# Attention of two layers: products with the values turned round, two heads side by side, two tiles of queries at a time

## The reference, cut to what matters

```python
def causal_block_attention(q, k, v, log_decay=None):
    ...
        logits = jnp.einsum('bhqd,bhkd->bhqk', qc, k).astype(jnp.float32)
        if log_decay is not None:
            logits = logits + args[2][..., None] - log_decay[:, :, None, :]
        q_idx = i * Q_BLOCK + jnp.arange(Q_BLOCK)
        logits = jnp.where(key_idx[None, :] <= q_idx[:, None], logits, -jnp.inf)
        p = jax.nn.softmax(logits, axis=-1).astype(v.dtype)
        return jnp.einsum('bhqk,bhkd->bhqd', p, v)
```

## Time and profile before

| | |
|---|---|
| median of 3 runs | 1582.45 us (1582.36 to 1582.68) |
| span of the profiled execution | 1580.1 us, 2.35 us under that median |
| PE busy | 1545.3 us, 98% of the span |
| DVE, ACT, POOL busy | 824.7, 736.3, 322.4 us |
| fox attention, products with the values | 493.7 to 576.0 us of the span |
| mla attention, the same | 1040.4 to 1160.6 us |

### The profile page before, as it was taken

The page is one execution under the profiler, slowest core; times in us unless marked ns, Lnnn a source line. Parts: engine busy times, 40 slices in busy tenths (PEclk is TensorE's granted clock), DMA queues, the critical chain, the costliest instruction groups (busy, mean ns, idle before and its releaser), DMA issues. The chain is left out here.

```text
span 1580.1 us, 22237 instructions
## 1 busy us (share of the span) xinstructions
PE 1545.3 (98%) x9054; PEld 1299.5 (82%) x9054; DVE 824.7 (52%) x1406; ACT 736.3 (47%) x1423; POOL 322.4 (20%) x273
## 2 busy tenths in 40 slices
PE   7999998999999999999999999999999999999999
PEld 6788787998898887788888888768887888888887
DVE  5355456556435755745334543668955644244442
ACT  4355445455654545544124443567845534133431
POOL 0000142001430001244013431032001343014420
PEclk9999999999999999999999999999999999999999
DMA  6202112323220103233223332110013333223331
GB/s 232 80 35 88 54 54 88 129 68 107 80 88 30 33 1 104 81 110 118 85 82 102 99 110 72 51 44 14 15 54 93 94 94 123 90 80 94 110 116 41
DMA packets 37462, 128.07 MB, mean 81 GB/s; under 512 B 4192, under 2 KB 8944, under 8 KB 37360
## 3 DMA queue, kind: packets, MB, share of 16 engines
q1 hardware_dynamic: 37360, 126.65, 25.3%
HBM read 124.54 MB, written 2.10 MB: 80 GB/s over the span
## 5 line engine op out<-in xcount | busy, mean ns | idle before, releaser
L321 PE MATMUL bank<-hhi,whi 128*128 128x512 f32 (+2 forms) x1064 | 419.4, 394 | 4.8 <-ACT hhi L1915 3.0
L323 PE MATMUL bank<-hhi,wlo 128*128 128x512 f32 (+2 forms) x1064 | 415.0, 390 | 0.0
L322 PE MATMUL bank<-hlo,whi 128*128 128x512 f32 (+2 forms) x1064 | 414.9, 390 | 0.0
L312 DVE TENSOR_TENSOR wlo<-wstage,whi 128x1024 fp32r<-128x1024 f32 (+9 forms) x250 | 278.6, 1117 | 129.4 <-ACT whi L302 129.0
L302 ACT CAST whi<-wstage 128x1024 fp32r<-128x1024 f32 (+9 forms) x250 | 236.1, 949 | 135.9 <-PE bank L323 131.2
L321 PEld LDWEIGHTS bank<-hhi,whi 128*128 128x128 f32 (+2 forms) x1064 | 199.2, 187 | 53.0 <-ACT hhi L1915 6.3
L2414 DVE SCALAR_TENSOR_TENSOR cr<-bank,vc,cr 128x511 f32<-128x511 f32 (+1 forms) x168 | 125.9, 749 | 217.1 <-ACT cr L2353 214.1
L323 PEld LDWEIGHTS bank<-hhi,wlo 128*128 128x128 f32 (+2 forms) x1064 | 199.0, 187 | 43.6
L322 PEld LDWEIGHTS bank<-hlo,whi 128*128 128x128 f32 (+2 forms) x1064 | 199.1, 187 | 41.4 <-issue 0.5
L2353 ACT ACTIVATE cr<-bank,vc 128x512 f32<-128x512 f32 x84 | 65.5, 780 | 248.5 <-PE bank L323 248.5
L2459 POOL TENSOR_TENSOR cr<-cr,cr 128x512 f32<-128x512 f32 x44 | 94.4, 2146 | 314.5 <-DVE cr L2414 279.8
(11 more groups left out here) (423 smaller groups left out, 2343.5 us busy)
## 6 DMA issues: line engine op xcount, KB each, us to landing
wstage<-in_wts SPq DMA_DIRECT2D x147, 512.0 KB, 3.6
wstage<-in_wts SPq DMA_DIRECT2D x32, 704.0 KB, 4.1
wstage<-in_wts SPq DMA_DIRECT2D x14, 768.0 KB, 4.3
xT<-in_x SPq DMA_DIRECT2D x4, 512.0 KB, 5.0
xt<-in_x SPq DMA_DIRECT2D x4, 512.0 KB, 6.6
out<-ob SPq DMA_DIRECT2D x8, 256.0 KB, 2.3
U<-in_rel_ext SPq DMA_DIRECT2D x6, 256.0 KB, 9.0
wstage<-in_wts SPq DMA_DIRECT2D x2, 603.0 KB, 3.8
```

Source lines behind the costliest of these rows:

```text
L312: e.tensor_tensor(K.wlo[i % 3][:, p], K.stage[i % 3][:, p], K.whi[i % 3][:, p].bitcast(F32), SUB).then_inc(*K.dve.up(("wlo", i) if last el ...
L321: e.matmul(o, lh, rh, start=start, stop=False)
L322: e.matmul(o, lh, rl, start=False, stop=False)
L323: return e.matmul(o, ll, rh, start=False, stop=stop)
```

## The change

For fox and mla (not for the first block's window attention, whose `lumps` is None) the product with the values is turned round, and put off until two tiles of queries of both heads are there. A "lump" is one part of a pair: tiles (0, 1) or tiles (2, 3) of both heads.

- In `lump` the values of a head (128 keys x 64) are loaded and the turned probabilities move: 256 queries at once, 128 at the one block of keys that only the second tile sees. Head 0 of the pair goes to the first 64 columns of the array and rows of the bank, head 1 to the other 64, alternating. The bank then holds the result already turned, 128 rows (two heads) x 512 queries.
- So the transposes of `y` go. In their place the inverse sums must be spread over 64 columns and turned: DVE inverts them at step last+3, POOL (`pool_att`, a stage program that is new) copies them with a broadcast into `y` (128x512), PE turns that at last+5 (`factors`, four transposes), ACT copies it back at last+6, and DVE multiplies the bank by it at last+7 in one 128x512 instruction. ACT's high part comes at last+8 and DVE's low part at last+9, both from SBUF.
- A lump has two buffers (one a head) of 10 blocks of 128, two such for fox and one of 2x4 blocks for its memory heads; mla uses several places in turn. The copies out of PSUM are as many and as wide as before, with blocks at a stride.
- The two stages are one step longer, and `out0` and `out1` begin where they did.

```diff
+    def lump_items(self, p, n):
+        return [self.item_at[2 * p + s, i] for s in range(2) for i in self.lumps(p)[n]]
...
     def post(self, t):
-        return self.done(t - 7) if self.gen else None
+        return self.done(t - 8) if self.gen else None
...
+    def lump(p, part):
+        tiles = A.lumps(p)[part]
+        if part == 0:
+            A.O.go_on_at(A.out_bank(p))
+            A.O.take(q, (A.name, "O", p))
+        b = K.bank((A.name, "O", p))
+        for t in sorted(A.lump_items(p, part)):
+            q.wait_ge(*K.at((A.name, "pt", t)))
+        keys = A.n(A.item_at[2 * p, tiles[-1]]) // P
+        for j in range(keys):
+            for s in range(2):
+                H = A.heads[2 * p + s]
...
+                i0 = max(j, tiles[0]) if H.width(0) == P else tiles[0]
+                n = tiles[-1] + 1 - i0
+                at = A.block(A.item_at[2 * p + s, i0], j)
+                z = e.matmul(b[64 * s:64 * s + 64, i0 * P:(i0 + n) * P], H.v(j), A.turned(A.item_at[2 * p, i0])[A.name, "pt", p, part][s][:, at:at + n, :],
+                             start=j == 0, stop=j == keys - 1)
...
+    def factors(p):
+        b = A.T.take(q, (A.name, "R", p))
+        q.wait_ge(*K.at((A.name, "rr over", p)))
+        for i in range(4):
+            z = e.transpose(b[:, i * P:(i + 1) * P], A.y[A.name, "y", p][:, i * P:(i + 1) * P], K.ident[:])
+        z.then_inc(*K.pe.up((A.name, "R", p)))
...
-        if 5 <= t <= N + 4:
+        if A.lumps is None and 5 <= t <= N + 4:
             pv(t - 5)
-        p = A.post(t)
-        if p is not None:
-            q.wait_ge(*K.at((A.name, "fin", p)))
-            b = A.T.take(q, (A.name, "yT", p))
-            for c in range(4):
-                z = e.transpose(b[:, c * P:(c + 1) * P], A.y[A.name, "y", p][:, c, :], K.ident[:])
-            z.then_inc(*K.pe.up((A.name, "yT", p), frees=[(A.name, "y", p)]))
+        if A.lumps and t - 5 in A.lump_end:
+            lump(*A.lump_end[t - 5])
+        if A.lumps and A.done(t - 5) is not None:
+            factors(A.done(t - 5))
...
+def pool_att(e, q, K, A):
+    for t in A.steps:
+        p = A.done(t - 3)
+        if p is not None:
+            y = A.y.take(q, (A.name, "y", p))
+            q.wait_ge(*K.at((A.name, "rr", p)))
+            q.wait_ge(*K.pool.last())
+            e.tensor_copy(y[:].rearrange("p (i h n) -> p h i n", i=4, h=2),
+                          A.rs[:, 2 * p:2 * p + 2, :].unsqueeze(3).to_broadcast([P, 2, 4, 64])).then_inc(*K.pool.up((A.name, "rr over", p)))
...
+        p = A.done(t - 7) if A.lumps else None
+        if p is not None:
+            y = A.y[A.name, "y", p]
+            q.wait_ge(*K.at((A.name, "pv", p)))
+            q.wait_ge(*K.at((A.name, "factors", p)))
+            e.tensor_tensor(y[:], K.bank((A.name, "O", p))[:], y[:], MUL).then_inc(
+                *K.dve.up((A.name, "fin", p), frees=[(A.name, "O", p)]))
...
-    out += ["out0"] + ["foxatt"] * 3 + ["out0"] * 7 + ["bar5"] + ["norm1"] * 2 + ["ffn0"] * 63 + ["bar6"] + ["norm2"] * 2
+    out += ["out0"] + ["foxatt"] * 4 + ["out0"] * 7 + ["bar5"] + ["norm1"] * 2 + ["ffn0"] * 63 + ["bar6"] + ["norm2"] * 2
```

More of the change, by code:

```diff
@@ L990, with __init__ @@
 class Attention:
-    def __init__(self, name, heads, rings, P, pt, st, mx, rs, out, gen=None, y=None, given=None, pta=None, out_bank=lambda p: p % 2):
+    def __init__(self, name, heads, rings, P, pt, st, mx, rs, out, gen=None, y=None, given=None, pta=None, out_bank=lambda p: p % 2,
+                 lumps=None):
         self.name, self.heads, self.pt, self.st, self.mx, self.rs = name, heads, pt, st, mx, rs
@@ L1010, in __init__, with lump_of, block @@
         self.last = [max(t for t, item in enumerate(self.items) if item[0] // 2 == p) for p in range(len(heads) // 2)]
-        self.given, self.pta = given, pta
-        self.steps = range(-2, len(self.items) + 8)
+        self.given, self.pta, self.lumps = given, pta, lumps
+        self.steps = range(-2, len(self.items) + (9 if lumps else 8))
+        if lumps:
+            self.item_at = {item: t for t, item in enumerate(self.items)}
+            self.lump_end = {max(self.lump_items(p, n)): (p, n) for p in range(len(heads) // 2) for n in range(len(lumps(p)))}
+            self.lump_begin = {min(self.lump_items(p, n)): (p, n) for p, n in self.lump_end.values()}
+    def lump_items(self, p, n):
+        return [self.item_at[2 * p + s, i] for s in range(2) for i in self.lumps(p)[n]]
+    def lump_of(self, t):
+        h, i = self.items[t]
+        return h // 2, [i in tiles for tiles in self.lumps(h // 2)].index(True)
+    def block(self, t, j):
+        h, i = self.items[t]
+        tiles = self.lumps(h // 2)[self.lump_of(t)[1]]
+        return len(tiles) * j + i - tiles[0]
     def n(self, t):
@@ L1033, in done, with blocks, turned @@
         return self.last.index(t) if t in self.last else None
+    def blocks(self, t):
+        at = [self.block(t, j) for j in range(self.n(t) // P)]
+        return [(0, at, slice(at[0], at[-1] + 1, at[1] - at[0] if len(at) > 1 else 1))]
+    def turned(self, t):
+        return (self.pt if self.pta is None or self.items[t][0] >= 4 else self.pta)
     def turned_on_act(self, t):
@@ L1122, in pe_att, with turned_tile @@
         yield
+def turned_tile(q, A, t):
+    p, part = A.lump_of(t)
+    if t in A.lump_begin:
+        A.turned(t).take(q, (A.name, "pt", p, part))
+    return A.turned(t)[A.name, "pt", p, part][A.items[t][0] % 2]
 def act_att(e, q, K, A):
@@ L1149, in act_att @@
             n = A.n(t - 3)
-            o = (A.pt if A.pta is None else A.pta).take(q, (A.name, "pt", t - 3))
-            act_evac(e, q, K, (A.name, "pt", t - 3), (A.name, "T", t - 3), o[:, 0:n], K.bank((A.name, "T", t - 3))[:, 0:n])
+            if A.lumps is None:
+                o = A.pt.take(q, (A.name, "pt", t - 3))
+                act_evac(e, q, K, (A.name, "pt", t - 3), (A.name, "T", t - 3), o[:, 0:n], K.bank((A.name, "T", t - 3))[:, 0:n])
+            else:
+                o, b = turned_tile(q, A, t - 3), K.bank((A.name, "T", t - 3))
+                q.wait_ge(*K.at((A.name, "T", t - 3)))
+                for j0, part, at in A.blocks(t - 3):
+                    z = e.copy(o[:, at, :], b[:, j0 * P:(j0 + len(part)) * P].rearrange("p (j n) -> p j n", j=len(part)))
+                z.then_inc(*K.act.up((A.name, "pt", t - 3), frees=[(A.name, "T", t - 3)]))
         if A.prep(t):
@@ L1159, in act_att @@
             e.activation(hi[0][:], K.bank((name, "T"))[0:96, :], ACT.Identity, scale=scale).then_inc(*K.act.up((name, "hi")))
+        p = A.done(t - 6) if A.lumps else None
+        if p is not None:
+            act_evac(e, q, K, (A.name, "factors", p), (A.name, "R", p), A.y[A.name, "y", p][:], K.bank((A.name, "R", p))[:])
         p = A.post(t)
@@ L1192, in finish @@
             e.reciprocal(rr, rr).then_inc(*K.dve.up((A.name, "rr", p)))
-            if A.y is not None:
-                A.y.take(q, (A.name, "y", p))
             q.wait_ge(*K.at((A.name, "rr", p)))
@@ L1204, in dve_att @@
             soft(t - late)
+        p = A.done(t - 3) if A.lumps else None
+        if p is not None:
+            rr = A.rs[:, 2 * p:2 * p + 2, :]
+            q.wait_ge(*K.at((A.name, "P", A.last[p])))
+            e.reciprocal(rr, rr).then_inc(*K.dve.up((A.name, "rr", p)))
+        p = A.done(t - 7) if A.lumps else None
+        if p is not None:
+            y = A.y[A.name, "y", p]
[3 more added lines that the diff above has]
+                *K.dve.up((A.name, "fin", p), frees=[(A.name, "O", p)]))
         p = A.post(t - 1)
@@ L1220, in dve_att @@
         for wait, tiles in ((6, (2, 3)), (5, (0, 1))):
-            if A.done(t - wait) is not None:
+            if A.lumps is None and A.done(t - wait) is not None:
                 finish(A.done(t - wait), tiles)
@@ L3094, in memory @@
         keys0 = sb("kt0", [P, 4, 4, 96], scope=s)
[L3095 removed]
+    K.parts = sb("parts", [P, 16, T])
     K.xT = sb("xT", [P, 8, T])
@@ L3187, in memory @@
     K.ff = [feed_forward(0)]
+    with above(0) as s:
+        seventh = Buffer(K, [sb("mla_seventh0", [P, 10, P], scope=s)], [(("mq", 7), "T"), (("mk", 7), "T")])
+        sb("below_seventh", [P, 256], scope=s)
+        seventh.t = (*seventh.t, sb("mla_seventh1", [P, 10, P], scope=s))
     with ExitStack() as s:
```

74 lines of the change are left out of this document (50 added, 24 removed).

## The result

The changed kernel takes 1591.22 us (median of 5 runs, 1584.96 to 1592.9), the kernel before 1582.36 in the runs beside it: a ratio of 1.0058, 95% interval 1.0039 to 1.0078. It is 9 us slower where I had forecast 24 us faster; 1591 lies outside my range of 1547 to 1575. The profiled execution of the change is its fastest run (1584.96 us, span 1583.2).

A forecast was written before the change was run, and what follows sets the result against it. PE, busy 98% of the span, was taken as the bound. Gains of 11.2 (fox), 8.7 (mla's causal heads) and 4.5 (memory heads) sum to 24.4 us: span 1555.7, 1558 by the median, range 1547 to 1575.

The forecast's parts named there:

- Products removed and added: PE in fox and mla: 65.7 us of products removed, cheaper lumps added; PE gives up 25.4 us.
- What is late next: Engines after the change: PE still bounds fox, 11.2 us less; three engines alike in mla's causal heads, 8.7 less.
- The other edits: Fox and mla: transposes nothing, DVE -0.2 a pair, one more ACT copy of 581 ns, POOL's copy 0.61 us.
- Memory heads: Mla's memory heads: 2.5 us of PE's work go, plus 2 for a wait and half clock; 4.5 in all.
- The factors' rival: Factors' transposes in PE's queue: late factors make PE wait about 1.5 us at each of 16 pairs; 1592, chance 0.07.
- The first rival: Causal pairs: lumps and DVE hold each other up, 12 us of 24.4 taken back; 1570, chance 0.18.
- the signs named: Traces, if wrong: last lump 3 us, PE idle over 10% of fox, POOL releasing PE, longer DVE copies, half clock.

The follow-up runs named there:

- e11_before_one_block: The kernel before, with only the first block of keys in each fox and mla product with the values: 1565.57 us, ratio 0.9903.
- e17_before_with_factors: The kernel before, with mla's chain of factors (DVE, POOL, PE, ACT) added and its copy read by nobody: 1592.55 us, ratio 1.0079.
- e15_before_finish_late: The kernel before, with mla's finish (from pair 2 on) and high and low parts one step later: 1583.14 us, ratio 1.0018.
- e1_no_factors: The changed kernel without PE's turn of the factors and ACT's copy; DVE multiplies by unturned factors: 1576.84 us, ratio 0.9974.
- e14_fox_only: The changed kernel with fox in the new form and mla in the form before: 1576.72 us, ratio 0.9982.
- e6_factors_other_bank: The changed kernel, with mla's turned factors from pair 2 on put into the idle bank of results: 1594.83 us, ratio 1.0091.

## Why the prediction was wrong, step by step

- **Products removed and added: right in size on PE.** The last lump took 1.66 us for 1.76, the halves overlap, DVE's copies with strided blocks keep their durations (663 to 691 ns for 128x512 in mla, 690 in the earlier trace rows for the low part). The Trainium skill's page TensorEngine Tiling (Key Properties) warned of a drain at each change of the array's mode; all that the lump leaves for it is 1.66 less its steps (3 x 0.43 + 0.22 = 1.51), 0.15 us.
- **"What is late next": this step failed, and it is about half of the miss.** I took what PE gives up as path time wherever PE was busy over 95%, and put 4% and 5.5% on the longest engine. In mla the loss on DVE is 25%. One block in place of all (`e11_before_one_block`) shows that 15.6 us of the old products' work were worth only 3.4 to 4.9 us of wall time in mla's causal stretch: my 8.7 us of gain were more than was there. A busy PE is part work and part tails of work it waited for; the share said nothing of how much could be taken away. The row has another number for this that I passed over: PE's weight loads were busy 69.31 of 80.0 us in mla's causal stretch, 87%, just as DVE with 86%. The Trainium skill's page Perfetto Trace Analysis (Identifying the Most-Contended Engine) says that matmul busy time is a poor measure and the weight loads' share a better one. Mla bears out the first half: 96% busy, and hardly anything to take. The second half these traces don't bear out: fox has 86% of weight loads too, with DVE at 70%, and there more could be taken. In fox 11.2 us were forecast, which is 76.5 us in the wider cut, one us above the floor at which fox stands with 19.0 us of the products' work gone. The new form's own gain there was 5.7, half of the 11.2.
- **"The other edits": mis-sized.** I priced the factors' chain as four transposes either way and one ACT copy of 0.58 us. The transposes were right as work. But the turn now takes a bank of turned probabilities for as long as ACT lets it lie, 3.15 us in the piece shown (1120.02 to 1123.17) and 0.57 more for the copy, and I did not ask who waits for that bank. In mla alone it costs 12.2 us of the whole (`e17_before_with_factors`), and leaving its middle out in both stages gives 13 to 14 back. The one step later at which a pair ends was priced at nothing; it costs 2.8 us of mla's causal stretch (`e15_before_finish_late`).
- **Memory heads: the wait went, the gain did not.** There is no wait of 2 us on `y` and no half clock in this execution's stretch (clock 1.00 for 0.92), yet it takes 43.9 us for 43.6. The chain's middle is 2.6 of that, both at full clock (43.9 against 41.3 in `e1_no_factors`); the 4.2 that it added to the kernel before may be in part the clock. Of the 4.8 us by which I missed this stretch, 2.2 stay unexplained. And the form before had lost up to 3.5 of its 43.6 us to the clock (0.08 x 43.6), so that getting the clock back gained nothing that shows.
- **The rivals.** The factors' rival had the right place and, at 1592, nearly the measured time, but the wrong wait: the transposes are on time (POOL's copy took 0.61 us, and PE never waits for POOL before line 1136); what is late is the copy behind them, one engine further. It had 0.07, and that its 1592 fits is luck: it came from a copy of 2.15 us that did not happen. The first rival, bursts that starve DVE, is refuted as the main cause. Of the signs named, PE idle over a tenth of fox, released by DVE, did not quite come: it was 9% (8.0 of 85.6), and the releaser was mostly ACT's exponential. Half clock inside one of the two stages did (mla, the rows at the end).
- **In sum** the three stretches miss by 33.6 us: fox 9.1, the memory heads 4.8, the causal heads 19.7. About 14 of it is gain on the products that was not there (8.7 in the causal heads, 5.5 in fox), about 11 the chain in these two (7.2 and 3.9), 2 to 3 the later end.

What stays open: how much of mla's loss is the clock itself, since no run holds it fixed; where the gain of `e14_fox_only` beyond fox comes from; and whether spreading or moving the lumps, or moving the chain's other instructions, would help at full clock. With the copy in front the change is still 0.3% slower than before; front copy and other bank together were not tried.

## What to carry to other kernels

Before pricing a saving on the busiest engine, cut that work out of the kernel as it is and time what is left: that floor, not the busy share, bounds what this order of work can gain. For every new step that borrows a shared bank, count from the taking to the release, through the queue of the engine that releases it, and name who needs the bank meanwhile. And where engines wait in a ring, a version that wins in one stage and loses in another is worth splitting: the change in fox alone is 0.2% faster, the whole change 0.6% slower.

## What the runs showed of the hardware

Two products in the two halves of TensorE's columns, 128 rows deep and with 64 columns of values each, run side by side at their full rate: 16 f32 records, 256 and 128 wide, in 1.66 us. Short pauses of a PE that is otherwise busy can be followed by some us at half clock. Windows of the changed kernel in mla:

```profile
1140.00:1144.00 4.00, 2.87 (x22) 2.13 (x21) 3.11 (x8) 2.23 (x7) 0.00 (x0) 1.00 0.01 2
...
1146.00:1149.00 3.00, 3.00 (x16) 1.96 (x15) 2.75 (x6) 2.36 (x8) 0.61 (x1) 0.50 0.52 175
```

The longest pause in them is 1.13 us. It does not always happen: two pauses of 1.13 and 1.14 us, 4 us apart, stand in this window, and the clock stays full.

```profile
1120.00:1130.00 10.00, 7.21 (x57) 6.04 (x56) 7.16 (x16) 7.26 (x21) 0.00 (x0) 1.00 0.00 0
```

In `e6_factors_other_bank` a wait of 5.9 us was removed, yet the whole took 1594.83 us against 1591.22; the clock, with up to 13.5 us, is large enough to explain it.
